# Embedding weights loaded once, and two of its steps placed elsewhere, at the end of each layer of a hybrid decoder

## The reference, cut to what matters

```
qry = (xt @ w_query).reshape(PEER_BLOCK, PEER_HEADS, 2, PEER_KEY_DIM)
... top 16 of 128 x 128 experts for each of 8 heads ...
act = jax.nn.gelu(jnp.einsum('td,thkd->thk', xt, expert_u[idx]))
return jnp.einsum('thk,thkd->td', gate * act, expert_v[idx])
...
x = x + peer_ffn(hf, ...)
x = x + jax.nn.sigmoid(rms_norm(x, ple_norm) @ ple_w_gate) * (pe @ ple_w)
```

## Time and profile before

| | |
|---|---|
| time, median of 3 | 4200.87 us |
| time of the profiled execution | 4196.88 us |
| its span, first to last instruction | 4194.8 us |
| mean granted TensorE clock | 0.946 |
| TensorE busy | 3743.3 us (89%) |
| VectorE busy | 2647.2 us (63%) |
| GpSimd busy | 1860.7 us (44%) |
| ScalarE busy | 734.3 us (18%) |
| HBM read | 1025.27 MB |

### The profile page before, as it was taken

The page is one execution under the profiler, slowest core; times in us unless marked ns, Lnnn a source line. Parts: engine busy times, 40 slices in busy tenths (PEclk is TensorE's granted clock), DMA queues, the critical chain, the costliest instruction groups (busy, mean ns, idle before and its releaser), DMA issues. The chain is left out here.

```text
span 4194.8 us, 42902 instructions
## 1 busy us (share of the span) xinstructions
PE 3743.3 (89%) x15498; PEld 2766.4 (66%) x15498; DVE 2647.2 (63%) x5548; ACT 734.3 (18%) x1375; POOL 1860.7 (44%) x1714
## 2 busy tenths in 40 slices
PE   8889998978999999994797899989789999999937
PEld 7546787867666666651685467878676666666516
DVE  4766215748677676877657652167486777668776
ACT  2243302212000000000222433022120000000002
POOL 6101103776455455556371020047664554555563
PEclk9889999999999999997898999999899999999968
DMA  3201134548999999999722011445599999999997
GB/s 104 111 30 41 57 137 115 125 120 299 409 409 409 409 402 410 406 409 397 274 83 111 31 41 67 141 119 123 131 311 410 409 406 407 409 408 407 402 391 267
DMA packets 333955, 1063.93 MB, mean 254 GB/s; under 512 B 79152, under 2 KB 96176, under 8 KB 312496
## 3 DMA queue, kind: packets, MB, share of 16 engines
q0 software_dynamic: 184320, 537.08, 34.8%
q1 hardware_dynamic: 132368, 505.22, 31.9%
q10 hardware_dynamic: 17056, 18.88, 1.3%
HBM read 1025.27 MB, written 35.78 MB: 253 GB/s over the span
## 5 line engine op out<-in xcount | busy, mean ns | idle before, releaser
L1665 PE MATMUL bank<-v_tile,shared 128*128 128x512 f32 x2048 | 908.4, 598 | 38.5 <-DVE shared L2041 35.3
L2100 POOL DMA_INDIRECT u_rows<-in_peer_u,idx_all x512 | 645.1, 1260 | 591.9 <-DVE act_u L1998 478.2
L2010 DVE SCALAR_TENSOR_TENSOR x<-v_rows,act_w,x 128x1024 f32<-128x1024 f32 x512 | 657.7, 1285 | 335.2 <-DMA v_rows<-in_peer_v,idx_all 316.9
L2100 POOL DMA_INDIRECT v_rows<-in_peer_v,idx_all x512 | 561.7, 1097 | 423.4 <-DVE x L2010 331.7
L1998 DVE CUSTOM_DVE_ANT_0 u_rows<-u_rows,h 128x1024 f32<-128x1024 f32 x512 | 610.9, 1222 | 189.9 <-DMA u_rows<-in_peer_u,idx_all 187.5
L1665 PEld LDWEIGHTS bank<-v_tile,shared 128*128 128x128 f32 x2048 | 392.5, 192 | 493.1 <-issue 447.2
L2110 POOL DMA_INDIRECT first_cells<-first_gate,cell_all x256 | 417.1, 1629 | 578.5 <-DVEq L1990 462.4
L1653 PE MATMUL bank<-hT,bT 128*128 128x256 f32 x2048 | 452.5, 379 | 0.0
L1653 PEld LDWEIGHTS bank<-hT,bT 128*128 128x128 f32 x2048 | 388.4, 190 | 72.0 <-issue 22.0
L1557 PE MATMUL bank<-hT,ring 128*128 128x256 f32 x1536 | 341.1, 383 | 14.2 <-PEq L150 14.2
L1557 PEld LDWEIGHTS bank<-hT,ring 128*128 128x128 f32 x1536 | 293.6, 192 | 56.5 <-issue 15.8
(11 more groups left out here) (375 smaller groups left out, 4749.8 us busy)
## 6 DMA issues: line engine op xcount, KB each, us to landing
v_tile<-in_peer_v SPq DMA_DIRECT2D x256, 512.0 KB, 7.5
ring<-in_w_in_panels SPq DMA_DIRECT2D x76, 1024.0 KB, 4.9
bT<-in_peer_ut SPq DMA_DIRECT2D x128, 512.0 KB, 7.9
ring<-in_peer_w_query SPq DMA_DIRECT2D x32, 1024.0 KB, 5.2
aT<-in_peer_ut SPq DMA_DIRECT2D x64, 512.0 KB, 6.9
sT<-in_peer_ut SPq DMA_DIRECT2D x64, 512.0 KB, 6.8
ring<-in_ple_w_gate SPq DMA_DIRECT2D x24, 1024.0 KB, 6.8
first_cells<-zeros SPq DMA_DIRECT2D x16, 1024.0 KB, 11.1
```

The lines of the kernel that those rows point to most:

```text
L1665: ins = mm(acc[t][part][:, :], act_pair[p % AHEAD][:, at:at + P], v_tile[:, e % DENSE, part * 512:part * 512 + 512], start=(e == 0), stop= ...
L2010: stt(out=m.x[:, 2 + t, :], in0=vr[:, n % RINGS, :], scalar=act_w[:, p % 4, i:i + 1], in1=m.x[:, 2 + t, :], op0=ALU.mult, op1=ALU.add).the ...
L2100: nc.gpsimd.indirect_dma_start(out=rows[:, n % RINGS, :], out_offset=None, in_=table, in_offset=bass.IndirectOffsetOnAxis(ap=idx_all[:, t, ...
```

## The change

Four things are done. The gate panels are loaded once for all units: three stay in the ring and the fourth goes, in halves, into `bT` and `query`, which are idle by then. The loads are issued from a new step `load_ple` after chunk 57, in which SP also issues those of the gain, `p` and `ple_w`. Unit 1 goes ahead of unit 0: `embed` after chunk 57, `scale` and `turn` after 58, its products from 59 on, with buffers of its own (`scores` and `h`). Unit 0's four products are all placed after chunk 61, and its first two `embedding` steps after chunk 64. Its last two stand behind `turned` of unit 2, and their sums lie in banks 6 and 7.

```diff
+LOADS_AT = 57
+SUMMED_AT = 64
...
-    after = {DENSE_END: [("add",), ("embed", 0)], DENSE_END + 1: [("scale", 0), ("turn", 0)], DENSE_END + 2: [("turned", 0)]}
-    for unit in range(2):
-        at = DENSE_END + 2 + 2 * unit
-        if unit:
-            after.setdefault(at - 2, []).append(("embed", unit))
-            after.setdefault(at - 1, []).extend([("scale", unit), ("turn", unit)])
-            after.setdefault(at, []).append(("turned", unit))
+    after = {LOADS_AT: [("load_ple",)]}
+    for unit, at in ((1, DENSE_END - 2), (0, DENSE_END)):
+        after.setdefault(at, []).extend([("add",), ("embed", unit)] if unit == 0 else [("embed", unit)])
+        after.setdefault(at + 1, []).extend([("scale", unit), ("turn", unit)])
+        after.setdefault(at + 2, []).append(("turned", unit))
         for n in range(4):
-            after.setdefault(at + n // 2, []).append(("embedded", unit, n))
-            after.setdefault(at + n // 2 + 1, []).append(("embedding", unit, n))
+            after.setdefault(at + 2 + (n // 2 if unit else 0), []).append(("embedded", unit, n))
+            if unit or n < 2:
+                after.setdefault(at + 3 + n // 2 if unit else SUMMED_AT, []).append(("embedding", unit, n))
...
-    order += [("sums",), ("embed", 2), ("scale", 2), ("turn", 2), ("turned", 2)]
+    order += [("sums",), ("embed", 2), ("scale", 2), ("turn", 2), ("turned", 2), ("embedding", 0, 2), ("embedding", 0, 3)]
...
             def embedded(unit, n):
...
-                w = panel()
+                if unit == 1 and n < RING:
+                    w_gate[n] = panel()
+                if unit == 1 and n == RING:
+                    pe.wait_ge(s.w_in, 16 * 2)
+                w = lambda k: w_gate[n][:, k, :] if n < RING else w_last[k // 4][:, k % 4, :]
...
-                panels.released.append((s.act_filled, to_act.n))
...
-                bank = to_vec.open()
+                side = unit == 0 and n >= 2
+                bank = m.banks[4 + n] if side else to_vec.open()
...
-            def add():
+            def load_ple():
+                for _ in range(RING):
+                    panel()
                 sp.wait_ge(s.hot_filled, QUADS)
...
+                sp.wait_ge(s.selected, PEER_HEADS)
+                for k in range(2):
+                    sp.dma_start(w_last[k], io.ple_w_gate[layer, RING][:, 4 * k:4 * k + 4, :]).then_inc(s.w_in, 16)
...
             def embedding(unit, n):
                 v.wait_ge(s.act_read, sig_count[unit, n])
...
-                if unit == 2:
+                if unit == 0 and n >= 2:
+                    v.wait_ge(s.side_sums, n - 1)
+                    step.step(tt(sig_of(unit, n), sig_of(unit, n), m.banks[4 + n][:, at], ALU.mult))
+                elif unit == 2:
```

More of the change, by code:

```diff
@@ L1490, in phase_tail @@
         ple_hT = comb
+        idle = scores[:, :, :, :, :].rearrange("p a t s k -> p (a t s k)")
+        early_hT = idle[:, 0:D].rearrange("p (k n) -> p k n", k=KD)
+        early_sig = idle[:, D:2 * D].rearrange("p (n c) -> p n c", c=PANEL)
+        w_last = [a.rearrange("p a n -> p (a n)").rearrange("p (k c) -> p k c", c=PANEL) for a in (m.bT[:, 2:4, :], qry[:, :, :])]
+        ple_rank = {2: 1, 0: 2, 1: 3, 3: 4}
+        normed_of = lambda unit, t: h[:, 0, :] if unit == 1 else ple_h[:, t, :]
+        turned_of = lambda unit, t: early_hT if unit == 1 else ple_hT[:, :, t * P:(t + 1) * P]
+        sig_of = lambda unit, n: early_sig[:, n, :] if unit else ple_sig[:, n, :]
+        stat = lambda unit, t, k: small[:, 25 + k:26 + k] if unit == 1 else small[:, 18 + 2 * k + t:19 + 2 * k + t]
         act_pair = [shared[:, k, :] for k in range(AHEAD)]
@@ L1669, in turn @@
             def turn(unit):
-                if unit == 0:
+                if unit == 1:
                     pe.wait_ge(s.pre_read, PAIRS_ALL)
                 for t, tile in zip(unit_at(unit), UNITS[unit]):
-                    pe.wait_ge(s.ple_h, tile + 1)
+                    pe.wait_ge(s.ple_h, ple_rank[tile])
                     for part, banks in ((0, to_act), (1, to_vec)):
@@ L1677, in turn @@
                             kk = 4 * part + k
-                            ins = nc.tensor.transpose(bank[:, k * P:(k + 1) * P], ple_h[:, t, kk * P:(kk + 1) * P], m.c("ident"))
+                            ins = nc.tensor.transpose(bank[:, k * P:(k + 1) * P], normed_of(unit, t)[:, kk * P:(kk + 1) * P], m.c("ident"))
                         ins.then_inc(banks.filled, 1)
@@ L1688, in sums @@
                 ins.then_inc(s.last_sums, 1)
+            w_gate = {}
             def embedded(unit, n):
@@ L1698, in embedded @@
                     for k in range(KD):
-                        ins = mm(bank[:, cols(t)], ple_hT[:, k, t * P:(t + 1) * P], w[:, k, :], start=(k == 0), stop=(k == KD - 1))
+                        ins = mm(bank[:, cols(t)], turned_of(unit, t)[:, k, :], w(k), start=(k == 0), stop=(k == KD - 1))
                 ins.then_inc(s.act_filled, 1)
-                panels.released.append((s.act_filled, to_act.n))
                 if unit == 2:
                     return
-                bank = to_vec.open()
+                side = unit == 0 and n >= 2
+                bank = m.banks[4 + n] if side else to_vec.open()
                 for t, tile in zip(unit_at(unit), UNITS[unit]):
@@ L1761, in add @@
                     sp.dma_start(w_ple[k], io.ple_w[layer, k * P:(k + 1) * P, :]).then_inc(s.p_in, 16)
+                sp.wait_ge(s.selected, PEER_HEADS)
+                for k in range(2):
+                    sp.dma_start(w_last[k], io.ple_w_gate[layer, RING][:, 4 * k:4 * k + 4, :]).then_inc(s.w_in, 16)
             loads = iter(range(len(sources)))
-            parts = {"gate": panel, "mix": panel, "out": panel, "query": panel, "embedded": panel, "pre": pre, "first_gates": first_gates,
-                     "values": values, "add": add}
+            parts = {"gate": panel, "mix": panel, "out": panel, "query": panel, "pre": pre, "first_gates": first_gates,
+                     "values": values, "load_ple": load_ple}
             for what, *n in order:
@@ L1853, in embed @@
                 for t, tile in zip(unit_at(unit), UNITS[unit]):
-                    squares = h[:, 0, :] if unit == 2 else ple_h[:, t, :]
-                    step.step(f(squares, m.x[:, tile, :], ACT.Square, accum_out=pss[:, t:t + 1]))
-                    f(prms[:, t:t + 1], pss[:, t:t + 1], ACT.Sqrt, bias=m.c("eps"), scale=1.0 / D).then_inc(s.ple_rms, 1)
+                    squares = h[:, 0, :] if unit == 2 else normed_of(unit, t)
+                    step.step(f(squares, m.x[:, tile, :], ACT.Square, accum_out=stat(unit, t, 0)))
+                    f(stat(unit, t, 1), stat(unit, t, 0), ACT.Sqrt, bias=m.c("eps"), scale=1.0 / D).then_inc(s.ple_rms, 1)
             def turn(unit):
@@ L1860, in turn @@
                     bank = banks.take()
-                    f(ple_hT[:, 0:4, t * P:(t + 1) * P], bank[:, :].rearrange("p (k n) -> p k n", k=4), ACT.Copy).then_inc(s.act_read, 1)
+                    f(turned_of(unit, t)[:, 0:4, :], bank[:, :].rearrange("p (k n) -> p k n", k=4), ACT.Copy).then_inc(s.act_read, 1)
             def embedded(unit, n):
-                if unit:
-                    act.wait_ge(s.ple_added, 4 * unit + n - 3)
+                if unit == 2:
+                    act.wait_ge(s.ple_added, 4)
                 bank = banks.take()
@@ L1870, in embedded @@
                 scale = prstd[:, unit_at(2)[0]:unit_at(2)[0] + 1] if unit == 2 else 1.0
-                f(ple_sig[:, n, at], bank[:, at], ACT.Sigmoid, scale=scale).then_inc(s.act_read, 1)
+                f(sig_of(unit, n), bank[:, at], ACT.Sigmoid, scale=scale).then_inc(s.act_read, 1)
                 sig_count[unit, n] = banks.n
@@ L2056, in scale @@
                         tt(ple_h[:, t, :], m.x[:, tile, :], gain[:, :], ALU.mult).then_inc(s.ple_h, 1)
-                        v.wait_ge(s.ple_rms, tile + 1)
+                        v.wait_ge(s.ple_rms, ple_rank[tile])
                         nc.vector.reciprocal(prstd[:, t:t + 1], prms[:, t:t + 1]).then_inc(s.last_scaled, 1)
                         continue
-                    v.wait_ge(s.ple_rms, tile + 1)
-                    step.step(nc.vector.reciprocal(prstd[:, t:t + 1], prms[:, t:t + 1]))
-                    stt(out=ple_h[:, t, :], in0=m.x[:, tile, :], scalar=prstd[:, t:t + 1], in1=gain[:, :],
+                    v.wait_ge(s.ple_rms, ple_rank[tile])
+                    step.step(nc.vector.reciprocal(stat(unit, t, 2), stat(unit, t, 1)))
+                    stt(out=normed_of(unit, t), in0=m.x[:, tile, :], scalar=stat(unit, t, 2), in1=gain[:, :],
                         op0=ALU.mult, op1=ALU.mult).then_inc(s.ple_h, 1)
@@ L2067, in turned @@
                     bank = banks.take()
-                    nc.vector.tensor_copy(ple_hT[:, 4:8, t * P:(t + 1) * P], bank[:, :].rearrange("p (k n) -> p k n", k=4)).then_inc(s.vec_read, 1)
```

(1 more changed line is left out.)

12 lines of the change are left out of this document (6 added, 6 removed).

## The result

The changed kernel takes 4209.75 us in the median of 20 runs, beside 4199.38 us for the kernel before: a ratio of 1.0023, 95% interval 1.0016 to 1.0030. The ratio leaves out one execution of the kernel before (6618.32 us) and two of the changed one (6248.73 and 4313.07), which were in a slower state. Timed once more beside other kernels it gave 1.0020 (1.0011 to 1.0029). It is slower, by 8 to 10 us, about what a measurement just tells from no change. The prediction was 4205.5.

What follows compares the result with a forecast made beforehand. VectorE was taken to bound layer 1 up to the first sum at 4120, then TensorE and VectorE by turns. Loads +2.4, products -1.2 and clock +1.1 gave +2.3 us a layer, +4.6 in all: 4205.5 us, range 4191 to 4213.

Steps and rivals of the forecast that it cites:

- loads: Before 4060, where DMA is full: the fourth panel's load delays the gathered rows, +2.4 us a layer, bounds 0 and 2.6.
- unit 1 first: VectorE's work for unit 1 and the bank wait make unit 0's products begin 6.7 us later a layer.
- clock at that start: At unit 0's first products: transposes close ahead regain 1.5 us of half-clock loss, bounds 0 and 2.1.
- the rest up to the start of the last products: From unit 0's fourth sigmoid to unit 2's products: -6.4 us; those products were to start 1.2 us earlier, at 4170.1.
- clock at the end: At unit 2's last products: TensorE idles some 12 us ahead, so 1.1 us is lost, between 0 and 2.1.
- The main step: Ahead of chunk 64: VectorE's 15 us of waits become one wait of 12 to 17 us for ScalarE's gelu.
- The late key blocks: Last two key blocks queue behind the load burst, landing near 4048 instead of 4021; a cover of 25 us hides it.
- the three signs of being wrong: Chunk 64 without wait, dense add waiting for TensorE, chunk 57's end to last add changing over 4 us a layer.
- the slower rival: Half clock at the first products of units 0 and 2, +11 us in all, 4212 us; chance 0.22.
- the forecast: The prediction's main case for the whole kernel: +2.3 us a layer, 4205.5 us; chance 0.64.
- The saved loads: Rival: the 8.4 MB saved after 4118 count, 20.5 us a layer, 4160 us; chance 0.04.
- The overlap that counts in full: Rival: chunk 64 waits for no gelu and TensorE's own work binds, -11.4 us a layer, 4178 us; chance 0.10.

Runs made afterwards that it cites:

- the fourth panel late: The changed kernel with the fourth panel's two half loads issued after chunk 59; 4204.26 us, ratio 1.0017 to the kernel before.
- loads alone: The changed kernel with its loads kept but units, products and sums in the order of before; 4203.00 us, ratio 1.0012 to the kernel before.
- the first burst warmed: The changed kernel with 16 unread products added on TensorE ahead of unit 0's last 12 transposes; 4203.49 us, ratio 1.0012 to the kernel before.
- the last burst warmed: The changed kernel with 27 unread products added on TensorE ahead of unit 2's transposes; 4201.83 us, ratio 1.0010 to the kernel before.

## Why the prediction came out as it did

The terms of a layer, as predicted, and as the profiles of before and after show them:

| term (from, to) | predicted | layer 0 | layer 1 |
|---|---|---|---|
| loads (chunk 53's weights, 58's) | +2.4 | +2.7 | +2.7 |
| unit 1 first (chunk 58's weights, unit 0's products) | +6.7 | +6.4 | +5.9 |
| clock at that start (products, fourth sigmoid) | -1.5 | +0.7 | +0.3 |
| the rest up to the start of the last products | -6.4 | -6.4 | -6.8 |
| clock at the end (last products, last add) | +1.1 | +1.8 | +1.7 |
| sum | +2.3 | +5.1 | +3.8 |

**The main step was right.** One wait for the gelu replaced the waits for products: 17.1 and 17.6 us where 12 to 17 was given. From the start of the fourth sigmoid to chunk 64's weights were 2.15 us in both layers, as predicted, and from there to the last products 18.2 for 18.6. This is shown, not only argued: with the two gelus put ahead of unit 0's last three sigmoids, and no other order changed, the stretch fell by 16.0 and 15.3 us.

**The loads were right**: 2.7 by the markers, 0.1 over the upper bound, and gone from there when one panel comes later. The late key blocks were hidden: the last dense pair ended at 4062.6 (4052.57 and 10.03), and the add of the banks began at 4093.6 without a wait, 31 us later. From chunk 57's end to the last add the layers changed by +2.4 and +1.1 us, within the 4 that were allowed, so none of the three signs of being wrong came.

**The step that failed** is "The clock at that start", as put: transposes stand close ahead, "I take 1.5" regained. Nothing was regained; the products took 9.3 to 9.6 us in all four layers of two profiles. The earlier trace rows was read as if the transposes had brought the clock back, and one place was taken for a rule. There the granted clock was 1.00 from 640 to 652 us and 0.57 from 652 to 656, so it had fallen only as the transposes began. The stretches of the end of the layer show that transposes close ahead are not enough. After:

```profile
4122.00:4126.00 4.00, 3.02 (x13) 2.61 (x12) 2.95 (x6) 2.26 (x4) 1.88 (x2) 0.50 0.93 311
4126.00:4130.00 4.00, 4.00 (x11) 3.15 (x10) 3.96 (x10) 1.11 (x1) 3.05 (x2) 0.50 0.86 302
```

and with the fourth panel late:

```profile
4118.00:4122.00 4.00, 2.82 (x12) 2.42 (x12) 2.70 (x7) 1.26 (x2) 2.71 (x3) 0.57 0.87 303
4122.00:4126.00 4.00, 3.48 (x16) 3.12 (x17) 4.00 (x8) 2.11 (x3) 2.02 (x2) 1.00 0.90 363
```

The same 2.82 us of transposes, the same gap of 1 us: with the fourth panel late the clock was back for the products, after the change it stayed at 0.50 until 4130. What decides between the two is not shown. The bounds, 0 and 2.1 regained, nearly held (0.3 to 0.7 was lost instead); one example was no reason to take a value near a bound.

**The clock at the end** was mis-sized: 1.7 to 1.8 for the 1.1 taken in the middle of 0 and 2.1. With both, the slower rival is what happened on TensorE: a granted clock of 0.5 in the first products of both bursts, and a time of 4209.75 and 4207.9 for its 4212. That rival was to decide from 1.9 us a layer over the forecast's sum; it was 2.8 and 1.5, or 2.15 in the mean. So it was the rival with 0.22 and not the forecast with 0.64. (The prediction's sentence on the Trainium skill calls it the second rival; in its list it is the third.)

The range held the time because it had been drawn to hold this rival too. By the prediction's own border, 8.4 us, the result is slower, to which it gave 0.24, and not the same (0.60). Part of the nearness of 4205.5 is luck: its base of 4200.87 lay 1.5 us above the 4199.38 measured beside the change, and the forecast's +4.6 on that gives 4204.0.

The rule of the Trainium skill that the prediction cited ("TensorE: Matmul & The Clock Gate", section "HAM oscillation — how this bites in real kernels"), that a burst behind an idle stretch starts slow, agrees with after: 9.44 for 7.07, and 15.79 for 14.07. It disagrees with the fourth panel late, where the first products took 7.14 behind 8.26 us of idle time and the transposes.

**The other rivals.** The saved loads count for nothing (loads alone: not faster but slower). The overlap that counts in full was priced at -11.4 a layer and 4178; with the gelus ahead, it measured -10.9 and -11.4, and 4174.85. Only its condition wasn't met.

## What to carry to other kernels

When work is moved off an engine's list of waits, follow the next thing that engine needs through the in-order queue that makes it: here a gelu of 0.2 us, queued behind four sigmoids, held VectorE for 17 us, and listing four products one or two chunks later took 16.0 and 15.3 us off the layers. A load that is saved where DMA has room pays for nothing that it adds where DMA is full. Price a burst behind idle TensorE at half clock unless the same place has been measured otherwise. Work put into the gap ahead of it may keep the clock, and that has to be measured: 16 added products did so ahead of unit 0's burst, 27 ahead of unit 2's did not in the execution that was profiled.

## What was not expected of the hardware

Twelve us of products at the full clock, up to 0.62 us ahead of eight transposes, did not keep it for the products 1.36 us behind these (12.21 us for 48), while 7 us of products, up to 0.21 us ahead of twelve transposes, kept it over a gap of 1.12 (7.14 for 32). The stretch around the transposes in the kernel with the first burst warmed:

```profile
4118.00:4122.00 4.00, 3.27 (x21) 2.47 (x19) 3.72 (x7) 0.90 (x2) 3.09 (x4) 1.00 0.94 316
```

TensorE was busy for 3.27 of its 4 us and the clock stayed at 1.00; in the kernel with the last burst warmed it was busy for 2.15 of 4, and the clock fell at their end. These are single places and give no rule. And a start at half clock has no fixed price: the same 32 products of unit 0 took from 8.71 to 9.90 us where the clock was at 0.50 as they began (7.14 where it was at 1.00), though the changed kernel repeated its own from 9.27 to 9.59.
